# Norms with one fused scaling and low halves by pairs of tiles, and other steps for merge gate pieces, weight splits and head sums in the third mixer's loop

## The reference, cut to what matters

```python
def modulate(x, shift, scale):
    return x * (1 + scale) + shift

def post_norm_update(x, y, gate, res_w, g, b):
    return layer_norm(DN_ALPHA * x + res_w * gate * y, g, b)
...
    # diff_attention, one block of queries
        s = jnp.einsum('bqhmd,bkhmd->bhmqk', qb, k)
        p = jax.nn.softmax(jnp.where(allowed, s, MASK_VALUE), axis=-1)
        w = p[:, :, 0] - lam * p[:, :, 1]
        return jnp.einsum('bhqk,bkhe->bqhe', w, v)
...
    o = _rms(o) * subln_g.astype(F32) * (1.0 - lambda_init)
...
    gates = jax.nn.sigmoid(mg.reshape(b, l, N_BRANCH, D_MODEL))
    y = jnp.sum(gates * y_b, axis=2)
```

## Time and profile before

| | |
|---|---|
| median of three runs (lowest, highest) | 3076.94 us (3074.57, 3077.59) |
| the profiled execution | 3072.28 us, span 3070.4 us |
| mean granted clock of TensorE | 0.984 of full |
| PE busy | 2936.9 us, 96% of the span |
| weight loads busy (beside PE) | 2577.1 us, 84% |
| DVE busy | 1752.0 us, 57% |
| ACT busy | 1377.8 us, 45% |
| POOL busy | 377.0 us, 12% |
| HBM | 155 GB/s over the span |

### The profile page before, as it was taken

The page is one execution under the profiler, slowest core; times in us unless marked ns, Lnnn a source line. Parts: engine busy times, 40 slices in busy tenths (PEclk is TensorE's granted clock), DMA queues, the critical chain, the costliest instruction groups (busy, mean ns, idle before and its releaser), DMA issues. The chain is left out here.

```text
span 3070.4 us, 51381 instructions
## 1 busy us (share of the span) xinstructions
PE 2936.9 (96%) x19512; PEld 2577.1 (84%) x19512; DVE 1752.0 (57%) x2586; ACT 1377.8 (45%) x1922; POOL 377.0 (12%) x306
## 2 busy tenths in 40 slices
PE   6999998999999999999899999999999999999998
PEld 3667765677888889888899989799999998988998
DVE  2323224266666656666545865657745577565784
ACT  1222213135655544554453553556644453536663
POOL 2111000122111110111100110101101002020110
PEclk9999999999999999999999999899999999999999
DMA  9986353741655654465435415245555451533564
GB/s 324 282 254 184 113 164 109 220 135 56 173 184 149 185 185 148 136 191 185 138 117 173 137 45 176 70 137 147 172 159 153 145 167 34 160 102 110 153 181 132
DMA packets 586156, 474.80 MB, mean 155 GB/s; under 512 B 28720, under 2 KB 547888, under 8 KB 585664
## 3 DMA queue, kind: packets, MB, share of 16 engines
q1 hardware_dynamic: 584464, 460.44, 49.0%
q0 software_dynamic: 1520, 11.95, 1.3%
HBM read 471.23 MB, written 4.72 MB: 155 GB/s over the span
## 5 line engine op out<-in xcount | busy, mean ns | idle before, releaser
L2263 DVE TENSOR_TENSOR low<-raw,high 128x1024 fp32r<-128x1024 f32 (+1 forms) x744 | 906.1, 1221 | 804.4 <-ACT high L2053 801.5
L2053 ACT CAST high<-raw 128x1024 fp32r<-128x1024 f32 (+1 forms) x744 | 768.5, 1034 | 1000.1 <-PE PS L1966 613.2
L1964 PE MATMUL PS<-NHh,high 128*128 128x272 f32 (+1 forms) x2304 | 668.8, 290 | 14.2 <-DVE NHl L1740 4.7
L1966 PE MATMUL PS<-NHh,low 128*128 128x272 f32 (+1 forms) x2304 | 661.1, 287 | 0.0
L1965 PE MATMUL PS<-NHl,high 128*128 128x272 f32 (+1 forms) x2304 | 660.2, 287 | 0.0
L1964 PEld LDWEIGHTS PS<-NHh,high 128*128 128x128 f32 x2304 | 433.4, 188 | 19.5 <-issue 15.4
L1965 PEld LDWEIGHTS PS<-NHl,high 128*128 128x128 f32 x2304 | 434.0, 188 | 0.8
L1966 PEld LDWEIGHTS PS<-NHh,low 128*128 128x128 f32 x2304 | 433.7, 188 | 0.0
L1962 PE MATMUL PS<-XX,high 128*128 128x512 f32 x966 | 347.7, 399 | 0.0
L1964 PE MATMUL PS<-XX,high 128*128 128x512 f32 (+1 forms) x752 | 274.4, 365 | 10.0 <-issue 5.7
L1961 PE MATMUL PS<-XX,low 128*128 128x256 f32 x966 | 271.6, 281 | 2.6 <-DVE XX L2299 2.6
(11 more groups left out here) (352 smaller groups left out, 4945.7 us busy)
## 6 DMA issues: line engine op xcount, KB each, us to landing
raw<-w_in_dram SPq DMA_DIRECT2D x416, 256.0 KB, 3.0
raw<-ffn_w_in_dram SPq DMA_DIRECT2D x352, 256.0 KB, 3.3
part<-ada_w_dram SPq DMA_DIRECT2D x184, 256.0 KB, 4.2
raw<-w_ffn_in_dram SPq DMA_DIRECT2D x176, 256.0 KB, 3.2
raw<-ffn_w_out_dram SPq DMA_DIRECT2D x160, 256.0 KB, 3.1
raw<-w_branch_dram SPq DMA_DIRECT2D x96, 256.0 KB, 3.1
raw<-w_ffn_out_dram SPq DMA_DIRECT2D x80, 256.0 KB, 3.0
part_sg<-ada_w_dram SPq DMA_DIRECT2D x48, 256.0 KB, 3.0
```

Source lines behind the costliest of these rows:

```text
L1964: nc.tensor.matmul(out, wh, xh, start=begin, stop=False)
L1966: last = nc.tensor.matmul(out, wl, xh, start=False, stop=end)
L2053: nc.scalar.copy(high[:, slot, 0:nk, :], raw[:, slot, 0:nk, :]).then_inc(s_high, 1)
L2263: nc.vector.tensor_tensor(low[:, slot, 0:nk, :], raw[:, slot, 0:nk, :], high[:, slot, 0:nk, :].bitcast(F32), ALU.subtract).then_inc(s_low, 1)
```

## The change

In the five norms with a modulation, DVE no longer standardises first. `scaled` multiplies TC by the column `ag` and by RS in one operation for each tile of 256 columns (twice for 512), without the shift. ACT's `x_high_pairs` adds the column `ab` while it writes XH, tile by tile. `x_low_pair` forms XL from TQ plus `ab` minus XH, pair by pair of tiles, and PE waits for each pair in front of its product. The standardising products follow behind, and ACT's residual passes wait for them by a new semaphore. In the third mixer's loop, pieces, fills and splits stand at steps that three tuples name; DVE's rotary step moves from step 4 to step 0; two of the four head sums move into PE's steps 20 and 21 and all four go to other banks (2 to 5, the meta sum to the end of bank 6); the first logarithm stands at ACT's step 22; for the last head the square stands ahead of the copy; ACT's sigmoids of the first two gate units stand behind the high parts, and DVE frees these units by the fill copies; unit 3 of the merge gate waits for the first logarithm alone, and the fillers wait for the second.

The diff, cut to one line of context:

```diff
@@ -423,7 +423,8 @@
         s_xh = sem("x_high_pairs")
-        s_xl = sem("x_low_halves")
+        s_xl = sem("x_low_pairs")
+        s_std = sem("standardised_halves")
         s_res = sem("residual_ready")
@@ -710,10 +711,10 @@
             act.wait_ge(s_oms, oms_first(layer, 2) + (2, 5)[half])
-            src = PS[:, 4 + 2 * half:6 + 2 * half, :].rearrange("p b (h t) -> p (b h) t", h=2)
+            src = PS[:, 2 + 2 * half:4 + 2 * half, :].rearrange("p b (h t) -> p (b h) t", h=2)
             last = nc.scalar.activation(rs[:, :, 0:SEQ], src, ACT.Ln, bias=bias, scale=scale)
             if half:
-                last = nc.scalar.activation(MI[:, 16:24, SEQ:T2], PS[:, 3, 0:P].rearrange("p (h t) -> p h t", h=DH),
+                last = nc.scalar.activation(MI[:, 16:24, SEQ:T2], PS[:, 6, 3 * P:4 * P].rearrange("p (h t) -> p h t", h=DH),
                                             ACT.Ln, bias=bias, scale=scale)
@@ -896,6 +897,9 @@
         DU = len(DA)
+        DA_PIECES = (1, 2, 6, 9, 13, 16, 19, 22)
+        DA_FILLS = (4, 11, 17, 23)
+        DA_SPLITS = (12, 14, 21, 23)
@@ -985,6 +989,11 @@
+            def head_sums(x):
+                pe.wait_ge(s_osq, hh0 + 2 * x + 2)
+                nc.tensor.matmul(PS[:, 2 + x, :].rearrange("p (h t) -> p h t", h=2), ones[:],
+                                 MI[:, 16 + 2 * x:18 + 2 * x, 0:SEQ], start=True, stop=True).then_inc(s_oms, 1)
             for t in range(DU + 6):
@@ -992,17 +1001,18 @@
                     transposes(t - 4)
-                if 2 <= t < 18 and t % 2 == 0:
-                    if t == 2:
+                if t in DA_PIECES:
+                    if t == DA_PIECES[0]:
                         pe.wait_ge(s_rope1, 24 * layer + 24)
-                    early((t - 2) // 2)
+                    early(DA_PIECES.index(t))
+                if t in (20, 21):
+                    pe.wait_ge(s_dx, u0 + DU)
+                    head_sums(t - 20)
             pe.wait_ge(s_dc, u0 + DU)
+            head_sums(2)
+            head_sums(3)
             pe.wait_ge(s_fill, 4 * (layer + 1))
-            for x in range(4):
-                pe.wait_ge(s_osq, hh0 + (7 if x < 2 else 8))
-                nc.tensor.matmul(PS[:, 4 + x, :].rearrange("p (h t) -> p h t", h=2), ones[:],
-                                 MI[:, 16 + 2 * x:18 + 2 * x, 0:SEQ], start=True, stop=True).then_inc(s_oms, 1)
-            nc.tensor.matmul(PS[:, 3, 0:P].rearrange("p (h t) -> p h t", h=DH), ones[:], MI[:, 16:24, SEQ:T2],
+            nc.tensor.matmul(PS[:, 6, 3 * P:4 * P].rearrange("p (h t) -> p h t", h=DH), ones[:], MI[:, 16:24, SEQ:T2],
                              start=True, stop=True).then_inc(s_oms, 1)
@@ -1040,25 +1050,29 @@
                     act.wait_ge(s_o, hh0 + h + 1)
-                    nc.scalar.copy(EX[:, h, :], PS[:, da_bank(h), 0:T2])
+                    if h < DH - 1:
+                        nc.scalar.copy(EX[:, h, :], PS[:, da_bank(h), 0:T2])
                     nc.scalar.activation(MI[:, 16 + h, :], PS[:, da_bank(h), 0:T2], ACT.Square).then_inc(s_osq, 1)
-                if t in (5, 9, 13, 17):
-                    x = (t - 5) // 4
+                    if h == DH - 1:
+                        nc.scalar.copy(EX[:, h, :], PS[:, da_bank(h), 0:T2])
+                if t == 22:
+                    tail_logs(act, layer, 2, 0)
+                if t in DA_FILLS:
+                    x = DA_FILLS.index(t)
                     if x % 2:
...
                     nc.scalar.copy(GR[:, x, :], PS[:, 6, 0:T2]).then_inc(s_fill, 1)
-                if 18 <= t < 22:
-                    early_split(t - 18)
-            early_gate(0)
-            early_gate(1)
-            for half in range(2):
-                tail_logs(act, layer, 2, half)
+                if t in DA_SPLITS:
+                    early_split(DA_SPLITS.index(t))
+            tail_logs(act, layer, 2, 1)
             for half in range(2):
...
                 tail_high(act, layer, 2, v)
+            early_gate(0)
+            early_gate(1)
@@ -1068,7 +1082,7 @@
             for t in range(DU + 4):
-                if t == 4:
+                if t == 0:
                     rope_dve(dve, s, (14, 15))
@@ -1096,10 +1110,10 @@
                     last.then_inc(s_dx, 1)
-                if t >= 19:
-                    early_split(t - 19)
+                if t in DA_SPLITS:
+                    early_split(DA_SPLITS.index(t))
+            early_gate(0)
             early_split(3)
-            early_gate(0)
             early_gate(1)
@@ -1919,8 +1933,6 @@
                         return
-                    if name in ("glu", "v", "cgate"):
-                        pe.wait_ge(s_xl, 2 * norms + c + 1)
                     if name == "branch":
@@ -1940,13 +1952,15 @@
                             if name == "mgate" and s["n"] == 2 and u == 3:
-                                pe.wait_ge(s_oln, half_first(s["layer"], 2) + 2)
+                                pe.wait_ge(s_oln, half_first(s["layer"], 2) + 1)
                         slot = (slot0 + c) % NSLOT
...
                             for k in range(nk):
+                                if name in ("glu", "v", "cgate") and (rolled(s) or not u) and j == 0 and k % 2 == 0:
+                                    pe.wait_ge(s_xl, 4 * norms + (k0 + k) // 2 + 1)
                                 wh = high[:, slot, k, j * P:(j + 1) * P]
@@ -2030,6 +2044,7 @@
                 if name == "mgate" and s["n"] == 2:
+                    pe.wait_ge(s_oln, half_first(s["layer"], 2) + 2)
                     keep_busy(pe, 7, 6)
@@ -2058,9 +2073,22 @@
+            def x_high_pairs(m, T):
+                for k in range(KT):
+                    act.wait_ge(s_modd, KT * m + k + 1)
+                    for c in range(T // SEQ):
+                        t = slice(c * SEQ, (c + 1) * SEQ)
+                        last = nc.scalar.activation(XH[:, k, t], TQ[:, k, t], ACT.Identity,
+                                                    bias=sm("ab", c)[:, k:k + 1])
+                    if k % 2:
+                        last.then_inc(s_xh, 1)
             def residual_rows(m, T):
...
                 for k in range(KT):
+                    if m < 5 and k % 4 == 0:
+                        act.wait_ge(s_std, 2 * m + k // 4 + 1)
                     dst = X[:, k, 0:T] if m < 5 else H[:, k, N_META:T2]
@@ -2209,7 +2237,7 @@
                     if m < 5:
-                        split_x_high(m + 1)
+                        x_high_pairs(m + 1, T)
                     else:
@@ -2297,13 +2325,26 @@
                 nc.vector.tensor_tensor(XL[:, k, 0:T], TQ[:, k, 0:T], XH[:, k, 0:T].bitcast(F32),
-                                        ALU.subtract).then_inc(s_xl, 1)
-
-            def modulate(m, src, T, before):
-                for hf in range(2):
-                    before(hf)
-                    modulated(hf, src, T)
-                    x_low(m, hf, T)
+                                        ALU.subtract).then_inc(s_xl, 2)
+            def scaled(hf, T):
+                for k in range(4 * hf, 4 * hf + 4):
+                    for c in range(T // SEQ):
+                        t = slice(c * SEQ, (c + 1) * SEQ)
+                        last = nc.vector.scalar_tensor_tensor(TQ[:, k, t], TC[:, k, t], sm("ag", c)[:, k:k + 1],
+                                                              RS[:, 1, t], ALU.mult, ALU.mult)
+                    last.then_inc(s_modd, 1)
+            def x_low_pair(m, v, T):
+                dve.wait_ge(s_xh, 4 * m + v + 1)
+                for k in (2 * v, 2 * v + 1):
+                    for c in range(T // SEQ):
+                        t = slice(c * SEQ, (c + 1) * SEQ)
+                        last = nc.vector.scalar_tensor_tensor(XL[:, k, t], TQ[:, k, t], sm("ab", c)[:, k:k + 1],
+                                                              XH[:, k, t].bitcast(F32), ALU.add, ALU.subtract)
+                last.then_inc(s_xl, 1)
@@ -2372,7 +2413,10 @@
             def early_free(u, s):
-                dve.wait_ge(s_act, s["act0"] + u + 1)
+                if s["n"] == 2:
+                    dve.wait_ge(s_fill, 4 * s["layer"] + 2 * u + 2)
+                else:
+                    dve.wait_ge(s_act, s["act0"] + u + 1)
                 dve.wait_ge(s_free, s["U0"] + u + 2)
@@ -2567,7 +2611,12 @@
                     if m < 5:
-                        modulate(m + 1, TC, T, lambda hf: link(standardise(hf)))
+                        for hf in range(2):
+                            scaled(hf, T)
+                            x_low_pair(m + 1, 2 * hf, T)
+                            x_low_pair(m + 1, 2 * hf + 1, T)
+                        for hf in range(2):
+                            standardise(hf).then_inc(s_std, 1)
                     else:
@@ -2663,7 +2712,7 @@
                     pool.wait_ge(s_free, U_end + 2)
-                    pool.wait_ge(s_xl, 4)
+                    pool.wait_ge(s_xl, 8)
                     pool.wait_ge(s_skew_out, 16)
```

## The result

The changed kernel takes 3046.38 us (median of 4 runs, 3043.65 to 3048.44) against 3075.76 for the kernel before in the same comparison: ratio 0.9907, 95% interval 0.9893 to 0.992. I had predicted 3046, between 3034 and 3062. The profiled execution took 3045.8 us, its span is 3044.0; against the span of 3070.4 before, 26.4 us are gone.

The account below looks back on a forecast made before the run. PE, busy 96% of the span, was taken as the bound, with waits in the norms and waits and low clock in the third mixer. Norms 14.2 plus mixers 17.0 gave 31.2 us saved: 3046 us, range 3034 to 3062.

Parts of the forecast that it names:

- 0.1 to 0.3 for clock lost behind the old waits: Narrow norms: extra gain where the clock fell behind PE's idleness, taken as 0.3 us in one norm and 0.1 in another.
- Cover for the second unit's gate sum: Narrow norms: the gate sum ends 0.4 us before PE wants its bank, costed at nothing; without cover 0.5 us per norm.
- rival (e): Norms: the fused form runs at half rate, so norms lose 13 us instead of winning 14; 3073 us, chance 0.03.
- I take 3.0 of 5.6: Wide norm: of 5.6 us won, 3.0 kept, since PE waits for ada_w parts with DMA at 0.95; range 0 to 5.6.
- rival (b): Norm gains are taken back at the second unit or on the DMA queue: 20 us in all, 3057 us, chance 0.05.
- Losses (1) and (2): Third mixer, first layer: PE's 2.51 us wait for DVE's sine product, and 1.2 us for the low-clock piece behind it.
- Loss (4): Third mixer, first layer: four head sums at low clock take 6.58 us instead of 3.6, so 3.0 us.
- Loss (3): Third mixer's last six steps: no piece left, PE waits for ACT's copies, small matmuls at half clock; 2.4 us.
- The allowance of 1.0 for splits in the middle: Third mixer's loop: splits at steps 12 and 14 hold DVE some 2.3 us with later weights queued behind; 1.0 us allowed.
- (a): Rival: DVE and ACT set the mixer's loop because splits stand inside it; 3 us a layer left, 3057 us, chance 0.12.
- (d): Rival: PE pauses in mixer steps without pieces and the whole middle runs at 1.2 GHz; slower, 3084 us, chance 0.04.
- (c): Rival: no mixer allowance is needed and the wide norm gives all: 40 us saved, 3037 us, chance 0.10.

Follow-up runs that it names:

- `rot4`: The changed kernel with DVE's last rotation back at step 4 and the first two pieces at steps 2 and 4: 3052.49 us, ratio 0.9922.
- `old_steps`: The changed kernel with the merge gate's eight pieces and four bank copies back at their steps of before: 3047.39 us, ratio 0.9907.
- `splits_late`: The changed kernel with the first two weight splits at loop steps 18 and 19 instead of 12 and 14: 3044.73 us, ratio 0.9898.
- `fill`: The changed kernel with filler matmul calls, seven ahead of the third mixer's last rotation and sixteen behind the sixth norm: 3048.08 us, ratio 0.9923.
- `halves`: The changed kernel with PE waiting for the low parts of x by four tiles instead of two: 3044.53 us, ratio 0.9896.
- `best`: The changed kernel with later bias loads, second split at step 15, fillers in idle places and fewer fillers in three others: 3042.88 us, ratio 0.9907.
- `splits15`: The changed kernel with the second weight split at loop step 15 instead of 14: 3046.89 us, ratio 0.9909.

## Why the prediction was right, and where not

**Narrow norms: right, under-sized.** 11.2 us forecast, 13.5 measured. The chain is as drawn, PE's start at +2.6 instead of +2.8, no wait inside. The term that was too long is the end of DVE's chain, and with it the end of the first unit (+9.3 forecast, +8.7 measured): +7.1 was forecast for the last low part, +6.4 came, because ACT's bias pass takes 0.40 us in sequence (four in 1.71) and not the 0.505 that I took from the residual passes, and DVE therefore never waits for it. I had also misread a chunk: between the rows lie 4.36 us, less 1.31 of waiting 3.05, where I wrote 2.8. After shows 3.03, so PE is the bound from its start on and wants no pair before it comes. And I had taken 0.1 to 0.3 for clock lost behind the old waits; before has 1.7 us of clock loss in the stages of the third and fourth of these norms, and yet all four stages give alike, so these terms were worth nothing. Cover for the second unit's gate sum held: no stage shows a new wait.

**The fused form.** Four of 256 columns take 1.67 us, one 0.48, so 0.40 us in sequence, against 0.41 forecast. The rule of the Trainium skill (Vector Engine (DVE) Microarchitecture Reference, Points that are easy to get wrong), by which two SBUF sources that are not bf16 halve the rate, is not borne out by these rows: rival (e) is dead.

**Wide norm: wrong in sign.** 3.0 us forecast, range 0 to 5.6; in the eight profiles of after's loads the stage is 0.0 to 3.8 us longer than in before. The step that failed is "I take 3.0 of 5.6". PE did start early: at 513.23, 5.0 us behind DVE's start (+5.1 forecast), after a wait of 2.22, and its second chunk at 520.03 (+11.8 for +11.9). So the 5.6 us were there, and I had asked only for the weight parts behind them. I did not follow POOL's queue, whose bias loads hang on the ends of units of the same product; that they come 8 to 9 us apart instead of 15.5 costs 4 to 5 us (249.6 against 244.4 to 245.6), more than the norm saves; part of that is clock lost behind the longer waits, a term that the forecast didn't have. This is a part of rival (b), for which I had no mechanism and gave 0.05. The range's lower end of 0 was wrong too: a gain ahead of a stage in which DMA runs at 0.95 can turn into a loss.

**Third mixer: right in sum, wrong in its bill.** 17.0 us forecast, 15.4 measured. In the loop itself the first layer came to 49.3 us (50.3 forecast), and a slow stretch ahead of it took 1.5 us of that back. Losses (1) and (2), the sine wait and the piece at half clock, are confirmed by `rot4`: 7.1 us over two layers, as expected. Loss (4), the head sums at half clock, went: 1.02 to 1.13 us for each of four, against 6.58 for all (4.3 in sum, 3.6 forecast). Loss (3) is where the reasoning failed. I had credited the pieces at steps 19 and 22 with ending the tail's waits and holding the clock. `old_steps` has no piece behind 16, 0.8 and 1.0 us more idleness, and its sum over both layers is within noise of after. The sums inside the loop and the two splits taken out of the tail may do the same work; that undoing one shows little would fit cures that overlap, but which of them would have done alone wasn't tried. The allowance of 1.0 for splits in the middle was right in size: of 2.5 us of waits for the masked scores, 1.5 stay in `splits_late`, where no split stands there. These 1.5 were in no term. The second layer fell short (6.6 of 8.0); its loop loses 3.4 us to the clock and the first layer's none. With that loss filled away (`fill`) its stage is 2.9 us shorter, though its waits in after are nearly the first layer's.

**Rivals.** (a) exists in small: the waits for DVE's masked scores, 2.5 and 2.7 us a layer, but PE stays the bound. (d) didn't occur: the granted clock is 1.00 throughout the first layer's loop; in the second, one stretch with 1.7 us of loss stands behind the rotation and one behind the wait of 1.31. (c) is false: neither the wide norm nor the mixer gave their upper ends.

**The sum.** 31.2 us forecast, 29.4 between the medians, 26.4 between the two profiled spans. That it came out so well is partly luck. By stages the parts of the change gave 13.5 - 3.8 + 15.4 = 25.1 us, 6.1 less than forecast: 2.3 too little for the narrow norms stand against 6.8 too much for the wide one and 1.6 for the mixers. In the profiled pair the start, 2.8 us earlier for no known reason, covers part of that; between the medians it is a wide stage that is usually nearer 249.6 than the profiled 252.5, and a start and a clock that vary. The shifts of about 1 us in untouched stages were in no term either.

## What to carry to other kernels

- Before taking a gain ahead of a stretch with the DMA engines near full, list every queue whose issues hang on the ends of units in it, the small loads on POOL included, and write down when each will now go out. Two transfers that were apart may meet.
- Where matmuls alternate with waits, sum the clock loss beside the idleness. Here PE's idleness fell by 1.7 and 2.0 us in the two mixer stages and their clock loss by 10.3 and 6.8; a bill made of waits alone would have found a quarter of the gain. But take the loss as a bound and not as time: where slow matmuls fill a wait, they cost nothing.
- Judge an edit by the lengths of stages between markers over several kernels, since a stage far away can take or give 1 to 3 us by clock alone; and size fillers by the busy time of a call, not by a row's count.

## What the runs showed of the hardware

- Granted clock: the same code with the same waits lost 5.1 us to half speed in the second layer's mixer in four kernels and 8.5 in a fifth (`halves`), and the stage behind the sixth norm 1.7 or 3.4. Fillers in the idle time take such a fall away at that place (1.00 instead of 0.66).
- A stretch with 1.7 us of clock loss lengthened the code ahead of the first layer's third mixer by 1.5 us (119.5 to 121.0), and two of the narrow norms' stages by nothing.
- Half-speed stretches of 8.5 us of loss also appear where PE is busy throughout (`best`, twice), in places where `fill` and `splits15` have short ones. No run here shows their cause.
- ACT's Identity pass of 128x256 with a bias alone follows its neighbour by 0.40 us, with bias and scale by 0.505; the second also writes plain float32, so the operands alone aren't isolated.
- The second group of bias loads beside the weight parts brought the DMA engines to a share of 1.06 over 15 us while PE waited 5.73 us for one part; without it they were at 0.79.
